# Column maxima added to the scores by matmuls on one half of the array's rows each

## The chip, the cores and the metric

The kernel runs on one core of a Trainium2 chip. The metric is the time of one execution on the device in microseconds (us); the time of the kernel before is the median of three runs.

## The reference

A decoder trunk of two layers, for 512 tokens of width 1024, in float32. Each layer has a token-mixing sub-layer and an MLP. The mixing sub-layer projects the normalised input once and feeds three attention branches: latent attention (MLA, 8 heads, causal), sliding-window attention with sinks (8 heads, in bands of two blocks of 128 keys) and stick-breaking attention (8 heads). The first two have a softmax, and the change is in how its maximum is taken off. What is computed is

```python
s = jnp.where(key_pos[None, :] <= q_pos[:, None], s, -jnp.inf)      # MLA, causal
p = jax.nn.softmax(s, axis=-1).astype(v.dtype)
...
m = jnp.maximum(jnp.max(s, axis=-1, keepdims=True), sink)           # sliding window
p = jnp.exp(s - m)
p = (p / (jnp.sum(p, axis=-1, keepdims=True) + jnp.exp(sink - m))).astype(v.dtype)
```

Any number that is at least about as large as the scores of a query would do as its maximum, since it is taken off in numerator and denominator alike.

## The kernel before

All activations lie transposed, with features or keys on the 128 partitions and the 512 tokens along the columns. Every float32 product is made of three matmuls, hi by hi, hi by lo and lo by hi, of operands split into a rounded part and a rest (`three`, L540 to L547). Weights stream through a ring of four buffers: SyncE issues the DMA (L528), ScalarE (ACT) rounds a chunk to `w_hi` (L991), VectorE (DVE) makes `w_lo` (L1533). The order of the tiles is written out by hand (`order`, L34, and the loops of each engine).

The scores of a head are transposed too: keys on the partitions, queries along the columns. A causal head has four pieces, one for each block of 128 keys with the queries that can see it, laid into three PSUM banks; a banded head has four pieces in two banks:

```python
CAUSAL = [(0, 0, 512, 0, 0), (1, 128, 384, 1, 0), (3, 384, 128, 1, 384), (2, 256, 256, 2, 0)]
BANDED = [(0, 0, 256, 0, 0), (1, 128, 256, 0, 256), (2, 256, 256, 1, 0), (3, 384, 128, 1, 256)]
```

with (key block, first query, columns, bank, column in the bank). A head then goes through these steps:

1. TensorE (PE) makes the scores and adds a mask (`scores`, L668, for MLA; `band_scores`, L760, two heads at once, one in each half of the rows). Each mask is a matmul by the identity through `add` (L549).
2. DVE takes the maximum of each partition over the pieces, into `mx` or `bmx` (`biggest`, L1622).
3. GpSimd (POOL) takes the maximum over the 128 partitions, so that every row of `mxr` or `bmxr` holds the maxima of all queries (`partition_all_reduce`, L2242 and L2219, mx_all). It takes 1.78 us.
4. PE subtracts them from the scores, in PSUM: `less_biggest` (L676). With all rows of `mxr` equal, a stationary matrix whose entries are all -1/128 (`NEG_PART`, made on L2273) gives minus the maximum in every row. There are four matmuls, one for each piece, of all 128 rows and 1280 or 896 columns in sum; the last of each bank counts up the semaphore `shift`.
5. ACT waits for `shift`, bank by bank, and makes the exponentials from each bank (`soft_exp`, L1066 to L1076), then their rounded part (`soft_hi`, L1078); DVE makes the rest (`probs_lo`, L1618, on L1620).
6. PE multiplies by the values (`values`, L693) once the rest is there (p_l) and the bank of the head before is free (pv_free).

The call for an MLA head, `mla_shift(h)`, stands in the middle of a projection tile (of `tile`, L586), after four of its eight input blocks: PE does twelve matmuls of that tile, then the call, then twelve more. Eight heads are called so. The banded heads follow in four pairs: `out_tile(0, n)` (L653, twelve matmuls), `band_shift(n)`, `out_tile(0, n + 1)`, `band_shift(n + 1)`, then a rotation or a tile, then `band_values(n)`, and the scores of the next pair. After the last pair come `stick_scores(0)` (L782), which wait for the exponentials of both heads, and `band_values(7)`. So there are 16 calls in a layer and 32 in all: 16 causal and 16 banded.

Others that wait for `shift` are POOL, ahead of the next reduction into the same buffer (L2217, L2241), and before it sets the ones beside the values (L2246).

Two places of the kernel before already use half of the rows for a matmul: `band_scores` (L768) and `stick_scores` (L799). There the heads of a pair alternate between rows 0 to 63 and rows 64 to 127, in different banks.

Of the kernel before, what the change touches and what calls it, by code (L numbers as in the profile page):

```python
# [12 lines left out]
P = 128  # L13
DEPTH, D, SEQ = 2, 1024, 512
HEADS, HEAD = 8, 64
# [104 lines left out]
IDENT, SWAP, NEG_TRI, NEG_ONE, ONE, MASK_CAUSAL, MASK_PREV, MASK_STRICT, NEG_PART, TRI01 = range(10)  # L120
# [4 lines left out]
BIG = 1e30  # L125
# [13 lines left out]
BANDED = [(0, 0, 256, 0, 0), (1, 128, 256, 0, 256), (2, 256, 256, 1, 0), (3, 384, 128, 1, 256)]  # L139
# [21 lines left out]
def trunk(nc, A_x, A_pos, A_w, A_vec, A_const, A_trig, A_first, out):  # L161
    x_spill = nc.dram_tensor("x_spill", (P, KT, SEQ), F32).ap()
    now = [0]
    with ExitStack() as ctx:
        at = [nc.sbuf_base + (-nc.sbuf_base) % 32]

        def place(name, shape, dt, offset=None):
            size = int(np.prod(shape[1:])) * 4
            if offset is None:
                offset = at[0]  # L170
                at[0] += size + (-size) % 32
            return nc.alloc_sbuf_tensor_at(name, shape, dt, offset=offset)
# [10 lines left out]
        cst = place("cst", [P, 9, P], F32R)  # L183
# [130 lines left out]
        def signal(name, per):  # L314
            return Signal(sem(name), per, now)
# [55 lines left out]
        shift = signal("score_shifted", 40)  # L371
# [130 lines left out]
        with nc.Block() as block:  # L502
# [35 lines left out]
            def _(pe):  # L538
# [10 lines left out]
                def add(o, stationary, moving):  # L549
                    return pe.matmul(o, stationary, moving, start=False, stop=True, skip_group_check=True)  # L550
# [124 lines left out]

                def less_biggest(n, pieces, banks, biggest_):  # L676

                    pe.wait_ge(*mx_all(n + 1))
                    for i, (j, q0, w, b, col) in enumerate(pieces):
                        mm = add(banks[b][:, col:col + w], cst[:, NEG_PART, :], biggest_[:, q0:q0 + w])  # L680
                        if i + 1 == len(pieces) or pieces[i + 1][3] != b:
                            mm.then_inc(shift.sem, 1)

                def mla_shift(h):
                    less_biggest(h, CAUSAL, score, mxr)

                def band_shift(n):
                    less_biggest(HEADS + n, BANDED, band[n % 2], bmxr[n % 2])
# [1579 lines left out]
def constants():  # L2268

    p, c = np.arange(P)[:, None], np.arange(P)[None, :]  # L2270
    swap = np.where(p % HEAD < HEAD // 2, p + HEAD // 2, p - HEAD // 2)
    mats = [p == c, swap == c, -(p >= c).astype(np.float32), -np.ones((P, P)), np.ones((P, P)),
            -BIG * (p > c), -BIG * (p <= c), -BIG * (p >= c), np.full((P, P), -1.0 / P), p < c]  # L2273
    const = np.concatenate([np.asarray(m, np.float32) for m in mats], axis=1)

    def inv(d):
        return (1.0 / (np.float32(THETA) ** (np.arange(0, d, 2, dtype=np.float32) / np.float32(d)))).astype(np.float32)

    row = np.arange(P)
    full, part = inv(HEAD)[row % (HEAD // 2)], inv(ROPE_DIM)[row % (ROPE_DIM // 2)]  # L2280
    sign_full = np.where(row % HEAD < HEAD // 2, -1.0, 1.0)
    sign_part = np.where(row % ROPE_DIM < ROPE_DIM // 2, -1.0, 1.0)
    q, one, zero = 0.25, np.ones(P), np.zeros(P)
    upper = row >= 3 * ROPE_DIM
    trig = [(full, q * one, one), (full, zero, sign_full),
            (part, np.where(upper, 0, q), np.where(upper, sign_part, 1.0)),
            (part, zero, sign_part)]
    cols = [v for f, ph, s in trig for v in (f, ph * 2 * np.pi, zero, s)]
    return const, np.stack(cols, axis=1).astype(np.float32)
# [77 lines left out]
```

## Time and profile before

| | |
|---|---|
| time, median of 3 runs | 1776.14 us (1775.68 to 1776.45) |
| the profiled execution | 1775.92 us |
| its span, first to last instruction | 1774.1 us |
| mean granted TensorE clock | 0.996 of 2.4 GHz |
| PE busy | 1743.8 us (98%) in 8734 matmuls |
| DVE, ACT, POOL busy | 1061.9, 843.9, 145.3 us |
| PE's share of the chain that ended last | 90% |

In the rows that follow, PE is the matmul and PEld the load of its stationary operand. Lines of the timeline give the start and the duration in us; a name with x4 behind it is a run of four that touch or overlap, and its duration runs from the first start to the last end. Matmuls are pipelined, so the duration of one (0.39 us for 512 columns) overlaps with the next; the distance between the starts of two tells what one costs. A bracket tells how long the engine was idle before the line and what ended the idle time.

### The profile page before, as it was taken

How to read it: one execution, taken by the hardware profiler on the slowest of the kernel's cores; microseconds unless marked ns; L12 is line 12 of the kernel's file. 1: busy time of each engine (PE TensorE's matmuls, PEld its weight loads, DVE VectorE, ACT ScalarE, POOL GpSimd, SP SyncE). 2: the span in 40 equal slices, each digit the busy share in tenths (PEclk: the TensorE clock that was granted, in tenths of full speed). 3: DMA queues.
4: the chain of work that ended last, by engine and by line, in shares of the span. 5: the costliest groups of instructions: out<-in, count | busy, mean ns of one | idle time of the engine just before them, and what ended most of it. 6: DMA issues, size and time to landing. Idle time of an engine off the chain costs nothing.

```text
span 1774.1 us, 21987 instructions
## 1 busy us (share of the span) xinstructions
PE 1743.8 (98%) x8734; PEld 1460.2 (82%) x8734; DVE 1061.9 (60%) x1428; ACT 843.9 (48%) x1187; POOL 145.3 (8%) x140
## 2 busy tenths in 40 slices
PE   8999999999999999999999999999999999999997
PEld 6888888888898888888888888888888988888886
DVE  7887876654557534354597777666554664343545
ACT  7575655554445414131466755655544553232223
POOL 0111221111200000000001112111111000000000
PEclk9999999999999999999999999999999999999999
DMA  4221112122342222222321221122124222222222
GB/s 152 66 79 60 60 60 70 62 72 77 117 140 72 96 95 95 95 95 96 110 86 63 75 72 48 60 72 71 62 82 154 84 95 95 94 97 95 95 93 74
DMA packets 47638, 152.37 MB, mean 86 GB/s; under 512 B 5296, under 2 KB 9776, under 8 KB 47536
## 3 DMA queue, kind: packets, MB, share of 16 engines
q1 hardware_dynamic: 45520, 147.02, 25.2%
q10 hardware_dynamic: 2016, 3.94, 0.6%
q8 instruction: 70, 1.15, 0.3%
q14 instruction: 32, 0.26, 0.0%
HBM read 146.75 MB, written 4.19 MB: 85 GB/s over the span
## 4 chain that ended last, share of the span: by engine, by line
PE 90%; DVE 5%; ACT 3%; issue 1%; DMA 1%; SPq 0%; POOL 0%; ACTq 0%; DVEq 0%
PE bank L545 83%; PE bank L550 4%; PE bank L839 1%; PE bank L799 1%; DVE w_lo L1533 1%; DMA x<-in_x 1%; DVE hf L1580 0%; DVE x L1589 0%; ACT dn L1048 0%; ACT dn L1046 0%; PE bank L649 0%; ACT w_hi L991 0%; DVE of L1652 0%; PE bank L554 0%; ACT h_hi L1027 0%
## 5 line engine op out<-in xcount | busy, mean ns | idle before, releaser
L545 PE MATMUL bank<-h_hi,w_hi 128*128 128x512 f32 (+1 forms) x1224 | 478.1, 391 | 6.2 <-DVE h_lo L1568 4.1
L545 PE MATMUL bank<-h_hi,w_lo 128*128 128x512 f32 (+1 forms) x1224 | 473.2, 387 | 0.0
L545 PE MATMUL bank<-h_lo,w_hi 128*128 128x512 f32 (+1 forms) x1224 | 473.0, 386 | 0.0
L991 ACT ACTIVATE w_hi<-raw 128x1024 fp32r<-128x1024 f32 (+2 forms) x269 | 271.1, 1013 | 228.8 <-DMA raw<-in_w 228.4
L1533 DVE TENSOR_TENSOR w_lo<-raw,w_hi 128x1024 fp32r<-128x1024 f32 (+2 forms) x269 | 316.8, 1181 | 65.1 <-ACT w_hi L991 58.8
L545 PEld LDWEIGHTS bank<-h_hi,w_hi 128*128 128x128 f32 x1224 | 230.7, 189 | 56.5 <-issue 7.0
L545 PEld LDWEIGHTS bank<-h_hi,w_lo 128*128 128x128 f32 x1224 | 230.6, 188 | 46.9
L545 PEld LDWEIGHTS bank<-h_lo,w_hi 128*128 128x128 f32 x1224 | 230.7, 189 | 44.9 <-issue 1.4
L545 PE MATMUL bank<-u_hi,w_hi 128*128 128x512 f32 (+1 forms) x560 | 211.4, 377 | 0.0
L545 PE MATMUL bank<-u_hi,w_lo 128*128 128x512 f32 (+1 forms) x560 | 211.0, 377 | 0.0
L545 PE MATMUL bank<-u_lo,w_hi 128*128 128x512 f32 (+1 forms) x560 | 211.0, 377 | 0.0
L545 PEld LDWEIGHTS bank<-u_lo,w_hi 128*128 128x128 f32 x560 | 105.6, 189 | 21.3
L545 PEld LDWEIGHTS bank<-u_hi,w_hi 128*128 128x128 f32 x560 | 105.6, 189 | 21.3
L545 PEld LDWEIGHTS bank<-u_hi,w_lo 128*128 128x128 f32 x560 | 105.6, 189 | 21.2
L1838 DVE TENSOR_TENSOR usq<-relu 128x512 f32<-128x512 f32 x64 | 44.3, 692 | 105.2 <-ACT relu L1195 104.7
L1195 ACT ACTIVATE relu<-bank 128x512 f32<-128x512 f32 x48 | 28.6, 596 | 140.3 <-PE bank L545 140.3
L1856 DVE TENSOR_TENSOR y<-bank,y 128x512 f32<-128x512 f32 x32 | 22.1, 692 | 104.5 <-PE bank L545 104.5
L545 PE MATMUL bank<-o_hi,w_hi 128*128 128x512 f32 x192 | 77.5, 404 | 0.0
L545 PE MATMUL bank<-o_hi,w_lo 128*128 128x512 f32 x192 | 76.2, 397 | 0.0
L545 PE MATMUL bank<-o_lo,w_hi 128*128 128x512 f32 x192 | 76.0, 396 | 0.0
L2230 POOL TENSOR_TENSOR mix<-mix,gate 128x512 f32<-128x512 f32 x32 | 44.4, 1392 | 367.9 <-DVE gate L1813 367.9
L1197 ACT ACTIVATE u_hi<-relu 128x512 fp32r<-128x512 f32 x64 | 40.5, 633 | 70.3 <-DVE relu L1833 68.8
(250 smaller groups left out, 2754.3 us busy)
## 6 DMA issues: line engine op xcount, KB each, us to landing
raw<-in_w SPq DMA_DIRECT2D x251, 512.0 KB, 3.3
x<-in_x SPq DMA_DIRECT2D x16, 256.0 KB, 3.7
side_raw<-in_w SPq DMA_DIRECT2D x6, 512.0 KB, 4.9
x_spill<-x ACTq DMA_DIRECT2D x8, 256.0 KB, 2.3
x<-x_spill SPq DMA_DIRECT2D x8, 256.0 KB, 3.3
out_y<-x SPq DMA_DIRECT2D x8, 256.0 KB, 2.2
raw<-in_w SPq DMA_DIRECT2D x8, 192.0 KB, 2.5
raw<-in_w SPq DMA_DIRECT2D x8, 128.0 KB, 2.4
```

The lines of the kernel that those rows point to most:

```text
L545: mm = pe.matmul(o, s, m, start=start and i == 0 and j == 0, stop=last and i == n - 1 and j == 2, skip_group_check=True)
L550: return pe.matmul(o, stationary, moving, start=False, stop=True, skip_group_check=True)
L799: mm = pe.matmul(to[:, off + col:off + col + w], a, m, start=off + col == 0 and i == 0, stop=i == 2, skip_group_check=True)
L839: mm = pe.matmul(pv_bank[:, q0:q0 + w], v[:, j, h % 2, :], part[:, s], start=i == 0 and part is p_hi, stop=part is p_lo, skip_group_check= ...
L991: act.activation(chunk_in(gc, w_hi, side_hi)[:, 0:w], chunk_in(gc, raw, side_raw)[:, 0:w], ACT.Copy)\
L1195: act.activation(relu[:, n % 2, :], tile_bank(name)[:, :], ACT.Relu).then_inc(free_of(name), 1)
L1197: act.activation(u_hi[g % 2][:, t, :], relu[:, n % 2, :], ACT.Square).then_inc(u_h.sem, 1)
L1533: dve.tensor_tensor(chunk_in(gc, w_lo, side_lo)[:, 0:w], chunk_in(gc, raw, side_raw)[:, 0:w], chunk_in(gc, w_hi, side_hi)[:, 0:w].bitcast( ...
L1838: dve.tensor_tensor(usq[:, n % 2, :], relu[:, n % 2, :], relu[:, n % 2, :], ALU.mult)\
L1856: ins = dve.tensor_tensor(y[:, t, :], tile_bank(name)[:, :], y[:, t, :], ALU.add)
L2230: pool.tensor_tensor(mix[:, t, :], mix[:, t, :], gated_at(b, t), ALU.add).then_inc(mix_add.sem, 1)
```

## The change

`less_biggest` is rewritten, and one constant with it. Each of the four matmuls now uses 64 of the 128 rows, of the stationary matrix and of the maxima alike: the pieces of the second bank (b == 1) rows 64 to 127, the others rows 0 to 63. The entries of the matrix become -2/128, so that 64 rows give minus the maximum. The banded pieces are taken in the order 0, 2, 3, 1, the causal ones as before, which puts the two halves of the rows next to each other in the queue. `shift` is counted up once in a call, by the last matmul, by the number of banks (3 or 2), and no longer by the last of each bank. There are as many matmuls and columns as before.

```diff
                 def less_biggest(n, pieces, banks, biggest_):
                     pe.wait_ge(*mx_all(n + 1))
-                    for i, (j, q0, w, b, col) in enumerate(pieces):
-                        mm = add(banks[b][:, col:col + w], cst[:, NEG_PART, :], biggest_[:, q0:q0 + w])
-                        if i + 1 == len(pieces) or pieces[i + 1][3] != b:
-                            mm.then_inc(shift.sem, 1)
+                    for i in ((0, 2, 3, 1) if pieces is BANDED else (0, 1, 2, 3)):
+                        j, q0, w, b, col = pieces[i]
+                        rows = slice(HEAD, P) if b == 1 else slice(0, HEAD)
+                        mm = add(banks[b][:, col:col + w], cst[rows, NEG_PART, :], biggest_[rows, q0:q0 + w])
+                    mm.then_inc(shift.sem, pieces[-1][3] + 1)
...
-            -BIG * (p > c), -BIG * (p <= c), -BIG * (p >= c), np.full((P, P), -1.0 / P), p < c]
+            -BIG * (p > c), -BIG * (p <= c), -BIG * (p >= c), np.full((P, P), -2.0 / P), p < c]
```

## Rows read from the trace of the kernel before

**Rows 1.** The page: busy time of PE, and the chain that ended last by engine
```profile
PE 1743.8 (98%) x8734; PEld 1460.2 (82%) x8734; DVE 1061.9 (60%) x1428; ACT 843.9 (48%) x1187; POOL 145.3 (8%) x140
...
PE 90%; DVE 5%; ACT 3%; issue 1%; DMA 1%; SPq 0%; POOL 0%; ACTq 0%; DVEq 0%
```

**Rows 2.** Groups of PE by shape: busy us, mean ns | idle before
```profile
L550 PE MATMUL bank<-bmxr,cst 128*128 128x256 f32 x48 | 8.8, 292 | 0.0
...
L550 PE MATMUL bank<-mxr,cst 128*128 128x512 f32 x16 | 6.5, 404 | 0.4 <-POOL mxr L2242 0.4
```

**Rows 3.** Timeline of a causal call, 62.0 to 63.2 us: start, duration, line
```profile
62.21 0.39 PE L545 MATMUL bank<-h_hi,w_lo 128*128 128x512 f32 x1
...
62.44 0.80 PE L550 MATMUL bank<-mxr,cst 128*128 128x512 f32 x4
62.87 0.60 ACT L1075 ACTIVATE s_f<-bank 128x512 f32<-128x512 f32 x1
...
63.08 0.39 PE L545 MATMUL bank<-h_hi,w_hi 128*128 128x512 f32 x1
```

**Rows 4.** Timeline of a banded call without a wait, 198.3 to 199.1 us
```profile
198.34 0.39 PE L545 MATMUL bank<-o_hi,w_lo 128*128 128x512 f32 x1
...
198.57 0.58 PE L550 MATMUL bank<-bmxr,cst 128*128 128x256 f32 x4
...
198.99 0.45 PE L756 MATMUL bank<-rp_hi,cst 128*128 128x512 f32 x1
```

**Rows 5.** Timeline of the one causal call that waits long, 144.5 to 146.3 us
```profile
144.58 0.39 PE L545 MATMUL bank<-h_hi,w_lo 128*128 128x512 f32 x1
145.41 0.70 PEld L550 LDWEIGHTS bank<-mxr,cst 128*128 128x128 f32 x4 [0.86 <-POOL mxr L2242]
...
146.15 0.39 PE L545 MATMUL bank<-h_hi,w_hi 128*128 128x512 f32 x1
```

**Rows 6.** Timeline of a banded call that waits for POOL, 213.7 to 214.7 us
```profile
213.79 0.40 PE L545 MATMUL bank<-o_hi,w_lo 128*128 128x512 f32 x1
214.01 0.54 PEld L550 LDWEIGHTS bank<-bmxr,cst 128*128 128x128 f32 x4 [0.26 <-POOL bmxr L2219]
...
214.54 0.45 PE L545 MATMUL bank<-o_hi,w_hi 128*128 128x512 f32 x1
```

**Rows 7.** Timeline, 286.6 to 287.5 us: from 128 rows to pairs of 64
```profile
286.75 0.39 PE L545 MATMUL bank<-h_hi,w_lo 128*128 128x512 f32 x1
287.07 0.19 PEld L799 LDWEIGHTS bank<-sb_hi 64*128 64x128 f32 x2 [0.35 <-issue]
...
287.18 0.19 PEld L799 LDWEIGHTS bank<-sb_lo,sb_hi 64*128 64x128 f32 x2
```

**Rows 8.** Timeline, 206.2 to 209.3 us: from pairs of 64 rows to 128
```profile
207.11 0.28 PE L768 MATMUL bank<-wq_hi,wk_lo 64*128 64x256 f32 x2
207.32 0.30 PEld L550 LDWEIGHTS bank<-cst 128*128 128x128 f32 x2
```

**Rows 9.** Timeline, 232.1 to 243 us: pairs of 64 rows in `stick_scores`
```profile
238.68 0.43 PE L799 MATMUL bank<-sb_lo,sb_hi 64*128 64x512 f32 x2
238.68 0.22 PEld L799 LDWEIGHTS bank<-sb_hi,sb_lo 64*128 64x128 f32 x2
```

**Rows 10.** Timelines: last step of the probabilities and first matmul of the values, two heads
```profile
66.37 1.49 DVE L1620 TENSOR_TENSOR p_lo<-s_f,p_hi 128x1280 fp32r<-128x1280 f32 x1
...
70.15 0.39 PE L545 MATMUL bank<-p_hi,mv_hi 128*128 128x512 f32 x1
...
138.47 1.49 DVE L1620 TENSOR_TENSOR p_lo<-s_f,p_hi 128x1280 fp32r<-128x1280 f32 x1 [1.33 <-ACT p_hi L1082]
...
140.10 0.45 PE L545 MATMUL bank<-p_hi,mv_hi 128*128 128x512 f32 x1
```

**Rows 11.** Timeline, 232.1 to 243 us: where PE waits after the last banded pair
```profile
238.37 0.50 PE L799 MATMUL bank<-sb_hi 64*128 64x512 f32 x2 [0.61 <-ACT bs_f L1075]
...
242.47 0.36 PE L545 MATMUL bank<-bp_hi,wv_hi 128*128 128x256 f32 x1 [1.27 <-DVE of L1652]
```

## The prediction

> **What bounds the kernel now.** I read the page first: PE is busy for 98% of the span, and the chain of waits that ended last lies on PE for 90% [rows 1]. So a nanosecond on PE's queue counts nearly fully, unless it falls into one of the few places where PE waits. The groups by shape then show the size of what is touched: 16 causal and 16 banded calls, of four matmuls each [rows 2] (48 of 256 columns is three in each of 16). Next the timeline of a call, where the distance between starts is the cost. A causal call puts 63.08 - 62.21 = 0.87 us between the tile's matmul before it and the one behind it [rows 3], of which 0.23 belong to the one before (62.44 - 62.21), so the four take 0.64 us. This is what their columns ask for (0.23, 0.17 and 0.11 for 512, 384 and 256) and a load or two of 0.11 that a short matmul doesn't cover. A banded call has 198.99 - 198.34 = 0.65 us between its neighbours [rows 4]. PE doesn't idle inside a call.
>
> Of the 16 causal calls 15 look as in [rows 3]; one waits for POOL and has 146.15 - 144.58 = 1.57 us [rows 5]. Of the 16 banded ones 10 look as in [rows 4]; four wait for POOL a little and have 214.54 - 213.79 = 0.75 us [rows 6], and two lie between, at 0.70.
>
> **The change, part by part.** *Halves at the same time.* What the change wants is that the lower rows stream beside the upper ones. The trace shows this in the kernel's own pairs: two matmuls of 64 rows and 256 columns end within 0.28 us together, no longer than one [rows 8]. For the causal order the upper rows have 512 and then 256 columns, the lower ones 384 and 128 in their shadow: the last piece starts 0.23 us after the first. In the banded order the upper rows have 256 and 256 beside 256 and 128: the last starts 0.12 us after the first, once the one ahead of it in the queue has begun.
>
> *The way into 64 rows and out of it.* Before, a load of all 128 rows runs beneath the matmul ahead of it. At a change from 128 rows to 64 it doesn't. Nothing else is in the way in [rows 7] (PE had been running tile after tile, and the operands had long been there), yet the load starts 287.07 - 286.75 = 0.32 us after the last full matmul's start, when all its columns are through and written, and the next load starts 0.11 later, which is when the first half matmul really streams: 0.43 us after the full one's start, where a neighbour of the same rows would stream after 0.23. The loss is 0.20 us. On the way back, from the start of the last pair to the full load is 207.32 - 207.11 = 0.21 us [rows 8], here between a head's scores and its mask, which has no wait at all, and the load takes another 0.11: 0.32 us, where 0.11 would do. The loss is again 0.20. The same distances stand at all changes of rows in the trace that have no wait, over thirty (shorter by what the columns take where the matmul before is narrower).
>
> Here the Trainium skill speaks against the change: its page TensorEngine Tiling (Tiling Modes, Key Properties) says that a change of the tiling mode drains the TensorE, without a price. Its page TensorE: Matmul & The Clock Gate (Part 3) gives the span of concurrent tiles as the duration of one matmul and some 4 ns for each further tile, and has no cost for getting into or out of tiles; a sum by that page alone is the first rival below. The rows decide for the first page.
>
> *Sum of a call.* Causal: 0.43 in, 0.23 to the last piece, 0.32 out = 0.98; the exact distances behind these roundings (0.425, 0.230, 0.310) give 0.97. That is 0.10 us more than the 0.87 of before. Fifteen calls: +1.5 us. In the waiting one [rows 5] the maxima come 0.83 us after the matmul before; the drain is over by then, so the way in is hidden: 0.83 + 0.11 + 0.23 + 0.31 = 1.48, against 1.57: -0.1. Banded: 0.43 + 0.12 + 0.31 = 0.86, so +0.21 for the ten as in [rows 4], +0.11 for the four as in [rows 6], whose wait of some 0.22 vanishes in the drain, and +0.16 for the two between: 2.1 + 0.4 + 0.3 = +2.8 us. All together: 1.4 + 2.8 = +4.2 us of PE's time.
>
> *One signal in place of two or three.* ACT began the first bank's exponentials at 62.87, 0.66 after the tile's matmul [rows 3]. Now it can begin only when the last piece is done: 0.43 + 0.23, a matmul's 0.28 and the step to ACT, 0.97. It is 0.3 later, and PE itself is 0.1 later, so the probabilities come 0.2 us nearer to their consumers. In the first head they are ready at 67.86 and used at 70.15 [rows 10]: 2.3 us of cover. All the other heads but one have at least a third of that. The tight one is the later pair of [rows 10], ready at 139.96 and used at 140.10; there the subtraction waits for ACT, whose own queue, not the signal, sets its start, so I cost it at nothing. In a banded call the signal comes about 0.1 to 0.2 later, no more than PE. Fewer increments gain nothing: the rows of before have no room for them between the matmuls. The constant costs nothing; it is loaded in the same way.
>
> *Where PE's loss is absorbed.* After the last pair, PE waits 0.61 us for the exponentials of the last head and then 1.27 us for DVE [rows 11]. Both chains go back through ACT's unbroken work to the exponentials of the head before, which begin at the signal of `band_shift(6)`; that signal comes 0.09 us later (two matmuls in sequence become a drain and one step). So instead of 0.11 + 0.21 for the two calls of this pair only 0.09 gets through: 0.23 us less, and that in each layer, 0.5 us. Elsewhere PE's waits hang on PE's own earlier work (scores, DVE, POOL), and move with it.
>
> The sum is 4.2 - 0.5 = +3.7 us against the profiled execution's 1775.92 us (a span of 1774.1 and 1.8 around it): 1779.6. The median of the runs shown, 1776.14, is 0.2 higher than that execution, which makes it 1779.9. A measurement of this kernel can tell some 0.2%, or 3.6 us, from no change; the forecast lies almost on that bound.
>
> **The rivals.**
> *No drain around short stretches* (the Clock Gate page's sum, faster). If a change of rows cost nothing, a causal call would take 0.23 + 0.23 + 0.12 = 0.58, 0.29 less, and a banded one 0.23 + 0.12 + 0.12 = 0.47, 0.18 to 0.28 less: 4.7 + 3.5 = 8.2 us, 1767.9. It decides where the two ways together cost less than the halves save: under 0.15 us each for the causal calls, 0.1 for the banded. The rows have 0.20 without an exception; only that these calls stand elsewhere speaks for it. Chance 0.07.
>
> *A late load in the other half* (slower). The last piece needs its load beneath the piece of the other half that is ahead of it in the queue. Such a load is in [rows 9]: it starts at 238.68 with the first matmul of the pair, while the second, which is ahead of it in the queue, starts at 238.72 (0.43 less 0.39 behind the first). The pairs there are of equal widths, though. If it had to wait, the last piece would be 0.06 late in a causal call, 0.11 in a banded one: 16 x 0.17 = +2.7, 1782.6. Chance 0.12.
>
> *The late signal becomes a wait*: 0.15 us in 16 causal calls is +2.4, 1782.3. The cover in [rows 10] speaks against it. Chance 0.05.
>
> *More is absorbed*: if the banded stretch is bound by DVE and ACT at more places than the last pair, half of its 2.8 us is lost there: +2.3, 1778.4. Chance 0.10.
>
> *The halves don't overlap* (the change doesn't do what it says): unequal widths run one behind the other. Causal 0.43 + 0.51 + 0.31 = 1.25, +0.38; banded 0.43 + 0.35 + 0.31 = 1.09, +0.44 less the waits; 12.4 less 0.5: 1788.0. Chance 0.04.
>
> **How the numbers follow.** The forecast has the remaining 0.62. Its own bounds are some 1 us to both sides (0.02 us at each of 32 calls, and the absorbed part between 0 and 1), so 0.37 of it lies over the bound of 0.2% and 0.25 under it. Slower: 0.37 + 0.12 + 0.05 + 0.04 = 0.58. Same: 0.25 + 0.10 = 0.35. Faster: 0.07. The range goes from 1777.4 to 1782.8: it takes in the forecast's bounds, the absorbed case and the two at 1782.3 and 1782.6, and leaves out the first and the last rival and some tails.
>
> **What would show it.** In the profile after, the loads of `mxr` and `bmxr` are 64 rows high and start 0.32 us after the full matmul before them, and from that matmul to the one behind the call there are 0.97 (causal) and 0.86 us (banded, the recorded start of the next being up to 0.11 earlier, since a matmul is recorded with its load after a drain). The first exponential of a causal head starts 0.97 after that matmul. PE's idle time, mostly under "issue", grows at these calls. PE's waits of 0.61 and 1.27 us shrink. Distances of 0.58 and 0.47 would make the first rival right, 1.25 and 1.09 the last; new waits of PE for p_lo the one of the signal.

## The result, and the profile after

The changed kernel takes 1779.41 us (median of 16 runs, 1777.91 to 1780.34), the kernel before 1776.17 us (16 runs, 1773.46 to 1778.02). The medians are 3.2 us apart; the ratio is 1.0015 with a 95% interval of 1.0008 to 1.0022: slower by 2.7 us, between 1.4 and 3.9. The profiled execution after took 1779.52 us, with a span of 1777.7 (before: 1775.92 and 1774.1); its mean granted clock is again 0.996.

The page of the changed kernel, to set beside [rows 1], and its groups of PE by shape (busy us, mean ns of one, idle before), to set beside [rows 2]:

```profile
PE 1747.4 (98%) x8734; PEld 1449.7 (82%) x8734; DVE 1061.8 (60%) x1428; ACT 844.2 (47%) x1187; POOL 145.7 (8%) x140
...
PE 90%; DVE 5%; ACT 3%; issue 1%; DMA 1%; SPq 0%; POOL 0%; ACTq 0%; DVEq 0%
```

```profile
L550 PE MATMUL bank<-bmxr,cst 64*128 64x256 f32 x48 | 8.0, 349 | 0.0
L550 PE MATMUL bank<-mxr,cst 64*128 64x512 f32 x16 | 7.9, 493 | 0.5 <-POOL mxr L2245 0.5
```

All four matmuls of a call now have 64 rows. PE carries the same share of the chain, with the same 8734 matmuls, and is busy for 3.6 us more. (Lines behind the changed function have moved on by three: L1075 is L1078 now, L1652 is L1655.)

The timeline of a causal call after, to set beside [rows 3] (start, duration, line, idle before):

```profile
76.11 0.39 PE L545 MATMUL bank<-h_hi,w_lo 128*128 128x512 f32 x1
...
76.43 0.30 PEld L550 LDWEIGHTS bank<-mxr,cst 64*128 64x128 f32 x4 [0.35 <-issue]
76.43 0.61 PE L550 MATMUL bank<-mxr,cst 64*128 64x512 f32 x4
76.97 0.19 PEld L545 LDWEIGHTS bank<-h_hi,w_hi 128*128 128x128 f32 x1 [0.24 <-issue]
76.97 0.50 PE L545 MATMUL bank<-h_hi,w_hi 128*128 128x512 f32 x1
...
77.21 0.60 ACT L1078 ACTIVATE s_f<-bank 128x512 f32<-128x512 f32 x1
77.31 0.40 PE L545 MATMUL bank<-h_lo,w_hi 128*128 128x512 f32 x1
...
78.00 0.39 PE L545 MATMUL bank<-h_lo,w_hi 128*128 128x512 f32 x1
```

Before, the load of the maxima's matrix ran beneath the full matmul. Now it stands behind it: 76.43 - 76.11 = 0.32 us, with 0.35 us in which no load is under way, put down to "issue", that is, to nothing that the profile shows. The four matmuls take 0.54 us by their records (76.97 - 76.43) where they took 0.64, so the halves do overlap. But the full load behind them again can't start beneath them. From the matmul before the call to the fifth one behind it there are 78.00 - 76.11 = 1.89 us, and the same around all calls like this one. In the kernel before it is 1.77 us (62.21 to 63.98; the second is the start of this row):

```profile
63.98 0.39 PE L545 MATMUL bank<-h_lo,w_hi 128*128 128x512 f32 x1
```

The call costs 0.12 us more by these rounded starts. The distances behind it go on growing by small parts: the cost is 0.10 us at the second matmul behind the call and 0.140 from the tenth on, in 14 of the 15 calls without a wait (0.133 in the last). ACT's first exponential starts 77.21 - 76.11 = 1.10 us after the tile's matmul in this head. In the first one, whose tile's matmul starts at 63.60, ACT had been free for 0.33 us, and it is the forecast 0.97; in most others it is 1.03, where it was 0.72 before:

```profile
64.57 0.60 ACT L1078 ACTIVATE s_f<-bank 128x512 f32<-128x512 f32 x1 [0.33 <-PE bank L550]
```

A banded call without a wait, after, to set beside [rows 4]:

```profile
201.12 0.40 PE L545 MATMUL bank<-o_hi,w_lo 128*128 128x512 f32 x1
201.44 0.30 PEld L550 LDWEIGHTS bank<-bmxr,cst 64*128 64x128 f32 x4 [0.36 <-issue]
201.44 0.50 PE L550 MATMUL bank<-bmxr,cst 64*128 64x256 f32 x4
...
201.87 0.50 PE L759 MATMUL bank<-rp_hi,cst 128*128 128x512 f32 x1
...
202.68 0.40 PE L545 MATMUL bank<-h_lo,w_hi 128*128 128x512 f32 x1
```

```profile
199.74 0.40 PE L545 MATMUL bank<-h_lo,w_hi 128*128 128x512 f32 x1
```

From 201.12 to 202.68 there are 1.56 us; before, whose row stands alone here, it was 1.40 (198.34 to 199.74), so 0.16 more (0.166 unrounded). The causal call that waits for POOL, to set beside [rows 5], hides its way in:

```profile
146.96 0.39 PE L545 MATMUL bank<-h_hi,w_lo 128*128 128x512 f32 x1
...
147.80 0.30 PEld L550 LDWEIGHTS bank<-mxr,cst 64*128 64x128 f32 x4 [0.88 <-POOL mxr L2245]
...
148.34 0.50 PE L545 MATMUL bank<-h_hi,w_hi 128*128 128x512 f32 x1
```

148.34 - 146.96 = 1.38 us by the records, and 0.11 more until the matmul behind streams: 1.49, where the prediction has 1.48.

**Where the 3.6 us of span come from.** I followed one matmul at the ends of the two stretches that hold the calls. After, the first causal call starts behind the first of these rows; the values after the last banded pair start at the second and fourth, and the third is the first call of layer 2:

```profile
63.60 0.39 PE L545 MATMUL bank<-h_hi,w_lo 128*128 128x512 f32 x1
...
245.71 0.36 PE L545 MATMUL bank<-bp_hi,wv_hi 128*128 128x256 f32 x1 [1.26 <-DVE of L1655]
...
941.44 0.39 PE L545 MATMUL bank<-h_hi,w_lo 128*128 128x512 f32 x1
...
1123.05 0.35 PE L545 MATMUL bank<-bp_hi,wv_hi 128*128 128x256 f32 x1 [1.27 <-DVE of L1655]
```

Before, they stand at 62.21 [rows 3], 242.47 [rows 11], and, in the timeline of layer 2:

```profile
938.27 0.39 PE L545 MATMUL bank<-h_hi,w_lo 128*128 128x512 f32 x1
...
1117.83 0.36 PE L545 MATMUL bank<-bp_hi,wv_hi 128*128 128x256 f32 x1 [1.27 <-DVE of L1652]
```

Layer 1 takes 182.11 against 180.26 us (+1.85), layer 2 181.61 against 179.56 (+2.05). The same cut at the last causal call gives +0.95 and +1.11 for the causal parts, +0.90 and +0.93 for the banded ones: **+3.9 us**, and nothing of note between the stretches. Beyond that the two profiled executions differ in the clock. After is already 1.39 us late at the first call, and before loses 1.6 behind 1117.83, where after loses nothing (5.22 us apart there, 3.6 at the end). The windows of both, first before, then after (stretch, its length, busy us of PE, PEld, DVE, ACT and POOL, granted clock, DMA share, GB/s):

```profile
22.50:26.00 3.50, 3.07 (x14) 2.20 (x13) 3.21 (x6) 3.11 (x4) 0.00 (x0) 1.00 0.00 0
1117.80:1122.30 4.50, 4.47 (x19) 4.02 (x20) 2.05 (x4) 0.42 (x1) 0.00 (x0) 0.62 0.02 4
```

```profile
22.50:26.00 3.50, 3.50 (x10) 2.70 (x10) 3.21 (x6) 3.45 (x4) 0.00 (x0) 0.54 0.00 0
...
1123.00:1127.50 4.50, 4.45 (x25) 3.95 (x26) 2.66 (x5) 1.07 (x1) 0.00 (x0) 1.00 0.00 0
```

A clock of 0.54 or 0.62 is a stretch that was mostly granted 1.2 GHz, the lower of the two levels. In the traces of the experiments such stretches stand in other places and in other numbers, so I take them for a part of the spread (4.6 us among the 16 runs before) and not of the change. There is one trace of each kernel, so that they move between executions of the same kernel is inferred, from the mean clocks of its runs (0.994 to 0.998 in the experiments). That is why I read the change from the two stretches of calls, and the total from the interval, whose upper end (3.9) the stretches reach. Runs with the same mean clock say the same: at 0.998 the change took 1777.91 to 1778.60 us (four runs), and the kernel before, beside the experiments, 1773.73 to 1774.85 (four runs), some 3.9 us less. The change's 16 runs had 0.9970 on the average, those of the kernel before beside the experiments 0.9960 to 0.9963, which fits a ratio that shows less than 3.9 us; the clocks of the 16 runs before are not known.

### The profile page after: what moved, and what is told of

Same layout as the page of the kernel before. It is cut to its first block, busy times and chain, and to the rows that moved or that the text cites. A ratio compares the mean times of both kernels' runs of the same rounds, so it can differ in the third digit from the quotient of the medians.

```text
span 1777.7 us, 21987 instructions
## 1 busy us (share of the span) xinstructions
PE 1747.4 (98%) x8734; PEld 1449.7 (82%) x8734; DVE 1061.8 (60%) x1428; ACT 844.2 (47%) x1187; POOL 145.7 (8%) x140
## 4 chain that ended last, share of the span: by engine, by line
PE 90%; DVE 5%; ACT 3%; issue 1%; DMA 1%; SPq 0%; POOL 0%; ACTq 0%; DVEq 0%
PE bank L545 83%; PE bank L550 4%; PE bank L842 1%; PE bank L802 1%; DVE w_lo L1536 1%; DMA x<-in_x 1%; DVE hf L1583 0%; DVE x L1592 0%; ACT dn L1051 0%; ACT dn L1049 0%; PE bank L649 0%; ACT w_hi L994 0%; DVE of L1655 0%; PE bank L554 0%; SPq L508 0%
```

## The experiments

In each, "growth" is the growth of the two stretches against the kernel before, in the order causal and banded of layer 1, causal and banded of layer 2. A ratio without another partner is against the kernel before, run on the same chip.

### One kind of call at a time

Only the causal calls are changed (`e1_causal_only`), or only the banded ones (`e2_banded_only`); the others keep 128 rows, a matrix of -1/128 of their own and the signals of before:

```diff
+                    if pieces is CAUSAL:        # e2: if pieces is BANDED
+                        for i in ((0, 2, 3, 1) if pieces is BANDED else (0, 1, 2, 3)):
+                            ...                 # as in the change
+                    else:
+                        ...                     # as before, with cst[:, NEG_FULL, :]
```

> The 16 causal calls are as in the change, the 16 banded ones as before (with a second constant of -1/128, one matrix more to load at the start). My theory (two drains of 0.20 us a call against what the halves save): from the full matmul before a causal call to the one behind it 0.86 us by the records, 0.97 with the load that the record hides, against 0.87 before; banded calls stay at 0.65 to 0.75. Sum of all causal calls +1.4 us, nothing absorbed, so +1.4 us (0.08%) against before, which five rounds can hardly tell from none. Rival (the late signal becomes a wait in the causal heads): +3 us or more, and new idle time of PE ahead of the matmuls by the values.

> The 16 banded calls are as in the change, the 16 causal ones as before. My theory: 0.76 us by the records (0.87 with the hidden load) against 0.65 to 0.75 before, +3.0 us of PE's time in all, of which some 0.5 are absorbed in PE's waits behind the last pair of each layer: +2.5 us (0.14%). Rival (more of the banded stretch is bound by DVE and ACT): +1 us or less, with PE's waits in that stretch shorter by more than 0.5 us in all.

Causal alone: 1778.5 us against 1776.78, ratio 1.0011 (1.0003 to 1.0020); growth 0.95, 0, 1.11, 0 = +2.07 us (unrounded), where I had expected +1.4. Banded alone: 1778.84, 1.0008 (1.0000 to 1.0017); growth 0, 0.92, 0.03, 0.93 = +1.88 us, where I had expected +2.5. The two add up to 3.95, the change's own 3.9 us. Neither part gains anywhere, and they don't act on one another. Each alone is smaller than what the timing can tell well; the stretches of the trace tell it.

### The single signal alone

The matmuls of before with all 128 rows, but `shift` counted up once, by the last:

```diff
-                        if i + 1 == len(pieces) or pieces[i + 1][3] != b:
-                            mm.then_inc(shift.sem, 1)
+                    mm.then_inc(shift.sem, pieces[-1][3] + 1)
```

> The matmuls are as before, of all 128 rows and in the old order; only the signal to ACT is given once, by the last of a call. My theory: the distances between the matmuls stay at 0.87 and 0.65 to 0.75 us, the first exponential of a causal head starts 0.25 to 0.3 us later behind the tile's matmul, and the time is the same within 0.5 us, because the probabilities have cover. Rival (the late signal costs): +1.5 to +2.5 us, with waits of PE for p_lo or POOL.

1777.32 us against 1776.78, ratio 1.0003 (0.9994 to 1.0012), no difference that the timing can tell. The trace has growth of 0.39, 0.19, 0.36, 0.18 = +1.12 us, more than the 0.5 that I had allowed and less than the rival's 1.5. Its timeline of the first causal call, to set beside [rows 3]:

```profile
62.12 0.39 PE L545 MATMUL bank<-h_hi,w_lo 128*128 128x512 f32 x1
...
62.99 0.39 PE L545 MATMUL bank<-h_hi,w_hi 128*128 128x512 f32 x1
...
63.19 0.60 ACT L1074 ACTIVATE s_f<-bank 128x512 f32<-128x512 f32 x1 [0.42 <-PE bank L550]
```

PE's 0.87 us stand, and the first exponential starts 1.07 us after the tile's matmul instead of 0.66. In the head with the tight cover, the later pair of [rows 10], it now is a wait:

```profile
138.78 1.50 DVE L1619 TENSOR_TENSOR p_lo<-s_f,p_hi 128x1280 fp32r<-128x1280 f32 x1 [1.32 <-ACT p_hi L1081]
...
140.33 0.19 PEld L545 LDWEIGHTS bank<-p_hi,mv_hi 128*128 128x128 f32 x1 [0.30 <-DVE p_lo L1619]
```

The rest is ready at 140.28, and PE's load starts at 140.33 after 0.30 us of idleness. ACT does start this head's exponentials without a gap behind its own work, as the prediction has it. But that work goes back, unbroken, to the exponentials of the head before, and those start when their signal comes:

```profile
123.68 1.36 ACT L1074 ACTIVATE s_f<-bank 128x512 f32<-128x512 f32 x3
...
136.10 0.58 ACT L1074 ACTIVATE s_f<-bank 128x512 f32<-128x512 f32 x1
```

In the kernel before these two stand at 123.36 and 135.79, while PE at this place is 0.09 us ahead of it here. So the signal of the head before, 0.4 us late, comes through after 12 us of ACT's queue. The other growth stands at the last causal call of layer 2, which comes to wait 0.52 us for POOL (1023.11), and at the values behind the last banded call of each layer, which come to wait for `bp_lo` (0.18 us each). In the change the signal is 0.3 us late, and PE itself loses 0.28 us in two calls, the one that gives that signal and the one behind it; its list of waits has no entry for p_lo.

### The signals bank by bank in the change

```diff
-                    mm.then_inc(shift.sem, pieces[-1][3] + 1)
+                        if pieces is not BANDED and i != 1:
+                            mm.then_inc(shift.sem, 1)
+                    if pieces is BANDED:
+                        mm.then_inc(shift.sem, 2)
```

> The changed kernel with the signals of the causal calls given bank by bank again. My theory: the first exponential of a causal head starts some 0.2 us earlier behind the tile's matmul (0.75 in place of 0.97), the distances between matmuls stay at 0.86 by the records, and the time is that of the change within 0.5 us, since in the change no matmul by the values waits for the probabilities. Rival (the signal is a part of the loss): 1 us or more faster than the change.

1778.3 us against 1776.32, ratio 1.0012 (1.0003 to 1.0021). Its timeline of the first causal call:

```profile
62.42 0.39 PE L545 MATMUL bank<-h_hi,w_lo 128*128 128x512 f32 x1
...
63.27 0.60 ACT L1081 ACTIVATE s_f<-bank 128x512 f32<-128x512 f32 x1 [0.22 <-PE bank L550]
63.28 0.19 PEld L545 LDWEIGHTS bank<-h_hi,w_hi 128*128 128x128 f32 x1 [0.24 <-issue]
```

ACT starts after 0.85 us (I had expected 0.75), and PE still needs 0.86 (63.28 - 62.42). Growth 0.81, 0.92, 1.11, 0.91 = +3.75 us against the change's 3.9. Most of the 0.15 us stands at one place, the call of layer 1 that waits for POOL (0.12 us shorter here). So the late signal of the causal calls is at most 0.15 us of the change's loss. The banded calls keep theirs in this run; their growth needs no late signal, since the calls' own costs (2.1 us, below) are more than it.

### All pieces in the upper rows

The change with its ways in and out, but with nothing in the lower half, so that no two matmuls can overlap:

```diff
-                        rows = slice(HEAD, P) if b == 1 else slice(0, HEAD)
+                        rows = slice(0, HEAD)
```

> The changed kernel with all four pieces on rows 0 to 63, so nothing runs side by side, and both drains stay. My theory: by the records some 1.14 us a causal call and 0.98 a banded one (0.11 more with the hidden load), that is +0.28 and +0.22 against the change: 8 us over the change, some 11.5 us over before. Rival (the halves gain nothing in the change, its cost comes from elsewhere): same time as the change.

1785.79 us against 1776.78, ratio 1.0047 (1.0032 to 1.0063); growth 2.73, 2.52, 3.09, 2.53 = +10.9 us, 7.0 over the change (11.5 and 8 expected). A causal call of its timeline:

```profile
75.07 0.39 PE L545 MATMUL bank<-h_hi,w_lo 128*128 128x512 f32 x1
...
75.39 0.70 PEld L550 LDWEIGHTS bank<-mxr,cst 64*128 64x128 f32 x4 [0.35 <-issue]
...
76.21 0.50 PE L545 MATMUL bank<-h_hi,w_hi 128*128 128x512 f32 x1
```

1.14 us by the records where the change has 0.86, and the same 0.32 us into the half rows. So the overlap is real and worth 0.28 us in a causal call (0.25 of it are left twelve matmuls on), 0.23 in a banded one; the ways in and out cost some 0.4 us and take more than that back.

### The banded pieces in plain order

This tests what the order is for, and the rule that I had for it, that matmuls begin in the order of the queue whatever rows they use. In plain order the second upper piece stands ahead of the first lower one:

```diff
-                    for i in ((0, 2, 3, 1) if pieces is BANDED else (0, 1, 2, 3)):
+                    for i in (0, 1, 2, 3):
```

> The changed kernel with the banded pieces in the plain order 0, 1, 2, 3: both pieces of the upper rows stand ahead of both of the lower. My theory (matmuls begin in the order of the queue, halves overlap only with their neighbours in it): by the records 0.88 us a banded call against 0.76 in the change, so +0.12 x 16 = +1.9 us of PE's time. Rival (each half runs its own pieces as they come): 0.76 and the same time.

1779.74 us against 1776.32, ratio 1.0015 (1.0006 to 1.0024); growth 0.95, 0.93, 1.11, 0.93 = +3.9 us, the change's own. A banded call of its timeline:

```profile
177.51 0.40 PE L545 MATMUL bank<-o_hi,w_lo 128*128 128x512 f32 x1
177.84 0.30 PEld L550 LDWEIGHTS bank<-bmxr,cst 64*128 64x128 f32 x4 [0.37 <-issue]
177.84 0.50 PE L550 MATMUL bank<-bmxr,cst 64*128 64x256 f32 x4
...
178.27 0.51 PE L545 MATMUL bank<-o_hi,w_hi 128*128 128x512 f32 x1
```

From load to load 178.27 - 177.84 = 0.43 us, as in the change (201.44 to 201.87). **My rule fell.** By it the second lower piece would start 0.23 us after the first upper one, 0.11 later than in the change. The single starts, by their unrounded times, show what happens: a second matmul begins 0.007 us behind the first upper one. Two of the same half stand 0.22 us apart (0.225 in `e4_upper_only`), so this is the first lower one, although another upper one is ahead of it in the queue. Each half works down its own pieces. The Trainium skill says otherwise (TensorE: Matmul & The Clock Gate, Part 3): there matmuls start and end strictly in program order, and only loads are pulled ahead. For the starts this case's trace does not agree. For the ends it shows nothing against it: the call's signal, given by the last matmul in the queue (128 columns, lower half), comes 0.534 us after the first start, behind the modelled end of the longer upper one (0.503).

### Fewer changes of rows elsewhere

If the way in and out is what costs, the kernel before should have time to win in `band_scores`, which goes from pairs of 64 rows to masks of 128 and back for each of two banks. I put the masks of both banks behind all pairs, two changes of rows in place of four, once in the kernel before (`e6_masks_last`) and once in the change (`e8_change_masks_last`):

```diff
                                           stop=i == 2, skip_group_check=True)
-                        if n % 2:
-                            ...                 # this bank's masks
+                    ...                         # the masks of bank 0, then those of bank 1
```

> The kernel before, with the masks of both banks in band_scores put behind all its half-row matmuls, so that each of its 8 runs has two changes of rows in place of four. The calls that take off the maxima are untouched. My theory (0.20 us a change): each band_scores is 0.40 us shorter on PE, 3.2 us in all; the first bank's signal comes some 0.3 us later, so a part goes into longer waits for POOL at the calls of the later pairs: -1 to -3 us against before. Rival (a change of rows costs nothing, the gaps there are the masks' own): no difference in PE's distances, and 0 to +1 us.

> The change and the masks of e6_masks_last together. My theory: the two add up; PE's distances are those of each alone, and the time is before +3.5 us less what e6_masks_last gains, about 1 to 2 us over before. Where e6_masks_last lost a part to waits for POOL at the calls, the drain of 0.32 us hides some of it here, so a little less than the plain sum is possible. Rival (the gains don't add): no faster than the change.

Neither gains, where I had expected -1 to -3 us and the sum of the two. `e6_masks_last`: 1777.16 against 1776.32, ratio 1.0003 (0.9994 to 1.0012), growth -0.04 us. `e8_change_masks_last`: 1779.84, 1.0017 (1.0009 to 1.0026), +3.86. The time is saved in its place, though: from the first load of `band_scores` to the last mask's start 2.46 us instead of 2.86, eight times, which makes 3.2. The list of PE's waits in `e6_masks_last` shows where it went (total us, times, longest), and the list of the kernel before below it:

```profile
PE bank L545 <- DVE of L1651: 6.8, 8, 1.3
...
PE bank L756 <- DVE rp_lo L1705: 1.4, 2, 0.7
```

```profile
PE bank L545 <- DVE of L1652: 4.4, 8, 1.3
...
PE bank L756 <- DVE rp_lo L1706: 0.6, 2, 0.3
```

2.4 and 0.8 us more, together the 3.2 saved. Behind the scores of a pair, PE waits for DVE, whose work on the head before frees the bank of the values (`pv_free`). This is a wait ahead of `band_values`, eight times, and a faster PE only arrives at it earlier.

### The values behind other work

That gave the next question: what if PE has something to do in that wait? In the kernel before I put `band_values(n - 1)` into the projection tile behind it, after three of its twelve matmuls, and `band_values(7)` into the tile of `stick_vt`, after six. The calls read so; inside `out_tile` and `tile` a new argument says where the values go:

```diff
-                        if t:
-                            band_values(n - 1)
-                        out_tile(0, n)
+                        out_tile(0, n, (lambda: band_values(n - 1)) if t else None, 1)
...
                     stick_scores(0)
-                    band_values(HEADS - 1)
-                    tile(("stick_vt", 0), h_hi, h_lo)
+                    tile(("stick_vt", 0), h_hi, h_lo, None, lambda: band_values(HEADS - 1), ALL, 2)
```

`e10_values_inside_masks_last` is this with the masks last, `e11_values_inside_change` this with the change, and `e12_last_values_inside` has only the second of the two moves.

> The kernel before, with PE's matmuls by the values of heads 1, 3 and 5 of the banded branch moved behind the first quarter of the output tile that followed them, and those of head 7 behind the first quarter of the tile that followed them. PE's waits for the product of the head before (of, 4.4 us in 8 places) are to be filled with three or six matmuls of the tile. My theory (these waits are the slack in which a gain of PE in band_scores was lost): they shrink to under 1 us in all and the time falls by 2 to 4 us, less what the later maxima of the next head add in waits for POOL. Rival (DVE and ACT bound this stretch as a whole): the waits turn up elsewhere, under banded maxima or the next tile, and the time is within 1 us of before.

> e9_values_inside and e6_masks_last together. My theory: with the wait behind band_scores filled, the 0.40 us that two changes of rows fewer save in each of 8 band_scores are no longer lost: 2 to 3 us below e9_values_inside, 4 to 7 below before. Rival (DVE and ACT bound the stretch): no faster than e9_values_inside.

> e9_values_inside with the change put on top. My theory: the causal calls cost what they did in the change, +2.1 us; of the banded ones those of heads 4 and 6 now wait for POOL longer than the drain lasts, so their way in is hidden and they cost nothing, the others +0.15 each: +3 to +4 us over e9_values_inside, 1776 to 1777. Rival (with other slack the change is free): within 1 us of e9_values_inside.

> The kernel before with one move of e9_values_inside alone: the matmuls by the values of head 7, behind stick_scores, go into the tile that follows them, so that PE no longer stands still for 1.3 us there. My theory: the place itself gives about 0.4 us a layer, and the clock of PE no longer falls behind that wait (0.62 of full in 4.5 us of the profile before), which gives up to 1.6 us once in most executions: -2 to -3 us against before, with less spread between runs. Rival (the gain of e9_values_inside is that of the moves within the pairs): -1 us or less.

| | us (lowest to highest of 11) | ratio to before |
|---|---|---|
| `e9_values_inside` | 1772.86 (1772.43 to 1773.49) | 0.9978 (0.9969 to 0.9987) |
| `e10_values_inside_masks_last` | 1772.9 (1772.48 to 1773.58) | 0.9979 (0.9970 to 0.9988) |
| `e11_values_inside_change` | 1775.98 (1775.51 to 1776.78) | 0.9998 (0.9989 to 1.0007) |
| `e12_last_values_inside` | 1774.16 (1773.55 to 1774.74) | 0.9987 (0.9978 to 0.9996) |

The kernel before took 1776.95 us beside the first two and 1776.56 beside the others. `e9_values_inside` beats both kernels, by 4.1 and, over the two comparisons, some 6.5 us. In its timeline the values of head 7 follow a tile's matmul without a bracket, 0.23 us behind it, where [rows 11] have a wait of 1.27, and in layer 2 no half-clock stretch follows, as the window shows (columns as above):

```profile
241.88 0.40 PE L545 MATMUL bank<-h_hi,w_lo 128*128 128x512 f32 x1
242.11 0.28 PE L545 MATMUL bank<-bp_hi,wv_hi 128*128 128x256 f32 x1
```

```profile
1116.00:1120.00 4.00, 4.00 (x25) 3.51 (x24) 2.02 (x5) 0.42 (x2) 0.00 (x0) 1.00 0.02 4
```

The 4.4 us of waits for DVE's `of` are gone. Of the 3.2 us by which the span is shorter (1774.1 to 1770.9), some 1.0 is won in layer 1 and 2.2 in layer 2, where 1.6 is the clock. Not all of the waiting is won: two waits of 1.3 us for another result of DVE come up a little later (0.4 us in all before), and four banded calls wait for POOL's maxima, 1.0 us in all (list of PE's waits):

```profile
PE bank L545 <- DVE tmp L1615: 2.5, 2, 1.3
...
PE bank L550 <- POOL bmxr L2220: 1.0, 4, 0.3
```

The masks last gain nothing on top of this either (1772.9, where I had expected 2 to 3 us less than `e9_values_inside`): the waits for POOL grow from 1.0 to 2.2 us and those for `rp_lo` from 0.6 to 1.4, which is 2.0 of the 3.2 us saved, so this stretch is in part bound by other engines behind the wait too. The rest I have not followed. The change costs 3.1 us here as well (1775.98 - 1772.86, in two comparisons), although two of its calls in each layer wait for POOL for longer than the way in lasts. The last move alone gives 2.4 us, of which its place in layer 1 shows only 0.43. In layer 2 its trace gains 1.6, about as much as the half-clock stretch costs that only the trace before has there. So most of its gain goes with the clock.

I did not try masks in half rows; no run here has two halves write the same bank.

## Why the prediction was right

1779.9 us was forecast and 1779.41 measured. Against the kernel before that is +3.7 forecast, +2.7 (1.4 to 3.9) by the interval and +3.9 in the trace. The mechanism held; that the sum came so close is in part luck, since its terms were off by +0.7, -0.7 and +0.3 us. And I had put 0.58 on a loss of more than 0.2%, 0.35 on a smaller difference: the loss measured is 0.15% (0.08 to 0.22).

*The way in and out*: right, and what decides it. The load starts 0.32 to 0.33 us behind the full matmul at every call without a wait, as in [rows 7]; `e4_upper_only` has the same 0.32 with no overlap at all. The Trainium skill's page TensorEngine Tiling (Tiling Modes, Key Properties) says that a change of the mode drains the TensorE, and this case's rows agree, with some 0.20 us lost each way. The first rival, the sum by the Trainium skill's page TensorE: Matmul & The Clock Gate (Part 3) with nothing for a drain, was 8.2 us faster than before; it falls.

*The halves at the same time*: right. The overlap is worth 7.0 us in sum (`e4_upper_only` less the change). The rival of halves that don't overlap falls.

*A late load in the other half*: the rival falls, and the sentence under it on which I rested the banded order with it. The step "once the one ahead of it in the queue has begun" was wrong: each half begins its pieces by itself. The number was not hurt, since in the order of the change both rules give 0.12 us; the order itself is worth nothing (`e5_plain_order`).

*Sum of a call*: the sign and the sum were right, both terms were mis-sized, in opposite directions. Causal: 0.10 forecast, 0.140 measured. The 0.10 stand at the second matmul behind the call; the matmuls from there to the tenth follow a little less closely than before, which adds the other 0.04. 15 calls make 2.1, not 1.5; the one that waits gains 0.03, not 0.1; and the stretches have 2.06. Banded: 0.21 forecast, 0.15 to 0.17 measured in calls like [rows 4]. In [rows 4] I took the start of the matmul behind the call, 198.99, as the start of its streaming. But the next one stands at 199.27, 0.28 us later and not 0.23: behind a matmul of 128 columns the record starts with the load's end in view, 0.05 early. The call before really took 0.70. By the same error the two calls between cost 0.11 instead of 0.16 and the four that wait 0.07 instead of 0.11; all the banded ones cost 1.6 + 0.3 + 0.2 = 2.1, not 2.8.

*Absorbed behind the last pair*: right in kind. The waits went from 0.61 to 0.49 us and from 1.27 to 1.26 in layer 1. The banded stretches grew by 0.90 + 0.93 = 1.83, so some 0.25 us of the 2.1 were absorbed, where I said 0.5; the rival by which half of the banded loss goes falls. Sum: 2.06 + 1.83 = 3.9 against my 4.2 - 0.5 = 3.7.

*The single signal at nothing*: nearly right in the change (at most 0.15 us, `e7_bank_signals`), for a reason that was half wrong. ACT's own queue does set the tight head's start, but that queue starts at the signal of the head before. With that signal 0.4 us late and PE not slowed, the tight head waited (`e3_signal_only`); in the change PE's own loss in the two calls, 0.28 us, covered most of the 0.3 us, and the 0.07 us by which the rest was ready ahead of PE's load covered the remainder. With PE kept at its old pace the single signal costs 1.1 us in the trace, so it is not free by itself.

## What to carry to other kernels

Matmuls of half the rows pay some 0.4 us for the way in and out together, so a short group of them amid full ones is worth it only where the overlap saves more than that, or where half-row work stands next to it already. Before a few tenths are saved on an engine, look for its next wait behind that place: `e6_masks_last` saved 3.2 us and gave all of them to a wait. And in this kernel the wait itself was the better object: filling it with matmuls that were ready gave 4.1 us with not one instruction fewer; in the traces half of the gain is the clock's.

## What the runs showed of the hardware

- The two halves of the rows are fed apart: a half-row matmul starts 0.007 us behind the first of the other half, though a second one of that other half is ahead of it in the queue (`e5_plain_order`). The signal of the last one in the queue still comes behind the modelled end of the other half's.
- A wait of PE of 1.27 us for DVE is followed in some executions, not in all, by a stretch at half the clock (a mean of 0.62 over 4.5 us at 1117.8), which costs 1.6 us on top of the wait. Of the ten traces whose kernels have this wait, three have such a stretch behind it in layer 2 alone (before, `e1_causal_only`, `e4_upper_only`), two in both layers (`e2_banded_only`, `e3_signal_only`), one in layer 1 alone (`e7_bank_signals`) and four in neither (the change, `e5_plain_order`, `e6_masks_last`, `e8_change_masks_last`). None of the four traces with the values inside has one, though PE waits as long there, a few us later, for another result of DVE. Another stretch stood at 22.5 us (0.54) in the execution after, where PE had stood still from 20.0 to 21.8. With the values inside, the runs spread by 1.1 us (`e9_values_inside`) to 1.3 (`e11_values_inside_change`), where the kernel before spreads by 3.6 to 4.7. What decides in which executions it happens stays open.
- After the way back to full rows the next two matmuls follow at 0.235 us, where they stand 0.227 apart in the kernel before. The same 0.236 stands behind an idle wait of that kernel (21.38 to 21.61), so it is not special to half rows. I have no cause for it.
